# A decoder layer's last eight down products: parts of 384 and 128 tokens in place of two halves of 256

## What is computed

```python
h = h + 0.5 * swiglu(rmsnorm(h, ffn2_norm[layer]), ffn2_w_gate[layer], ffn2_w_up[layer], ffn2_w_down[layer])
...
h = rmsnorm(h, final_norm)
return h[:, N_META:]
```

## Time and profile before

| | us |
|---|---|
| median of 3 runs (lowest, highest) | 1050.07 (1049.4, 1050.22) |
| the profiled execution, its own time | 1049.71 |
| its span, first to last instruction | 1048.0 |
| TensorE busy in the span | 1036.8 |
| VectorE / ScalarE / GpSimd busy | 741.8 / 501.9 / 589.5 |
| the stage of the last eight down products | 1014.67 to 1039.84 of the span |

### The profile page before, as it was taken

How to read it: one execution, slowest core, us unless ns; L and a number is a source line. 1 busy time by engine, 2 the same in 40 slices (tenths; PEclk the granted TensorE clock), 3 DMA queues, 4 the chain that set the end, 5 groups by cost and what they waited for, 6 DMA issues and landing times.

```text
span 1048.0 us, 20252 instructions
## 1 busy us (share of the span) xinstructions
PE 1036.8 (99%) x7723; PEld 961.8 (92%) x7723; DVE 741.8 (71%) x1271; ACT 501.9 (48%) x838; POOL 589.5 (56%) x695
## 2 busy tenths in 40 slices
PE   9999999999999999999999999999999999999997
PEld 9999999999999999879867787778899999999997
DVE  7547786566675588699875584578988876776735
ACT  6444455445354354562455526454554553554435
POOL 5945776575564367269821304356767755655740
PEclk9999999999999999989999999999999999999999
DMA  7245455555554444336311101222444655555532
GB/s 204 86 111 143 112 125 133 141 125 128 151 127 104 133 116 116 85 101 160 84 42 42 42 21 61 81 71 81 115 114 119 162 136 143 146 116 151 126 77 81
DMA packets 188772, 115.52 MB, mean 110 GB/s; under 512 B 7939, under 2 KB 178998, under 8 KB 188678
## 3 DMA queue, kind: packets, MB, share of 16 engines
q1 hardware_dynamic: 178208, 97.38, 33.0%
q0 software_dynamic: 10368, 16.78, 9.5%
q10 hardware_dynamic: 102, 0.08, 0.1%
HBM read 91.18 MB, written 2.10 MB: 89 GB/s over the span
## 4 chain that ended last, share of the span: by engine, by line
PE 94%; DVE 2%; issue 1%; ACT 1%; POOL 0%; DMA 0%; DVEq 0%; ACTq 0%; POOLq 0%
PE ps L2563 44%; PE ps L2784 34%; PE ps L617 4%; PE ps L2599 2%; PE ps L806 1%; PE ps L755 1%; PE ps L785 1%; PE ps L923 1%; PE ps L2835 1%; PE ps L2810 1%; PE ps L964 0%; POOL wl L1862 0%; PE ps L698 0%; DMA wxl<-raw 0%; DVE mask L1411 0%
## 5 line engine op out<-in xcount | busy, mean ns | idle before, releaser
L1862 POOL TENSOR_TENSOR wl<-raw,wh 128x256 fp32r<-128x256 f32 x292 | 248.0, 892 | 200.3 <-ACT wh L1997 165.2
L1884 POOL DMA_DIRECT2D wxl<-raw x72 | 60.7, 843 | 188.4 <-ACT wxl L2002 188.4
L2563 PE MATMUL ps<-ah,wxh 128*128 128x264 f32 (+2 forms) x464 | 123.2, 319 | 0.6 <-DMA wxl<-raw 0.6
L2563 PE MATMUL ps<-ah,wxl 128*128 128x264 f32 (+2 forms) x464 | 123.0, 318 | 0.0
L2563 PE MATMUL ps<-al,wxh 128*128 128x264 f32 (+2 forms) x464 | 122.8, 318 | 0.0
L2563 PE MATMUL ps<-xh,wh 128*128 128x264 f32 (+3 forms) x432 | 122.2, 334 | 0.2 <-DVE pja L1505 0.2
L1862 POOL TENSOR_TENSOR wxl<-raw,wxh 128x256 fp32r<-128x256 f32 x112 | 109.6, 1012 | 19.2 <-ACT wxh L1997 19.2
L2563 PE MATMUL ps<-xl,wh 128*128 128x264 f32 (+3 forms) x432 | 117.9, 324 | 0.0
L2563 PE MATMUL ps<-xh,wl 128*128 128x264 f32 (+3 forms) x432 | 117.7, 324 | 0.0
L2328 DVE SCALAR_TENSOR_TENSOR h<-ps,h 128x528 f32<-128x528 f32 (+1 forms) x88 | 61.0, 695 | 62.0 <-PE ps L2563 61.5
L1997 ACT ACTIVATE wxh<-raw 128x512 fp32r<-128x512 f32 (+2 forms) x88 | 53.6, 609 | 105.1 <-PE ps L2563 103.1
(11 more groups left out here) (326 smaller groups left out, 3004.0 us busy)
## 6 DMA issues: line engine op xcount, KB each, us to landing
raw<-in_ffn_w_gate SPq DMA_DIRECT2D x44, 512.0 KB, 4.4
raw<-in_ffn_w_up SPq DMA_DIRECT2D x44, 512.0 KB, 4.7
raw<-in_ffn_w_down SPq DMA_DIRECT2D x80, 256.0 KB, 2.8
wxl<-raw POOLq DMA_DIRECT2D x56, 256.0 KB, 3.6
raw<-in_w_in SPq DMA_DIRECT2D x28, 512.0 KB, 4.4
raw<-in_w_out SPq DMA_DIRECT2D x8, 512.0 KB, 3.4
xin<-in_x SPq DMA_DIRECT2D x4, 512.0 KB, 5.9
raw<-in_ffn_w_down SPq DMA_DIRECT2D x16, 128.0 KB, 2.2
```

What stands on the lines that cost most here:

```text
L1862: op = pool.tensor_tensor(dst[:, part], src[:, part], high[:, part].bitcast(F32), ALU.subtract)
L1884: pool.dma_start(places(1, PLACE[u], 1)[:, 0:n], raw[:, u % RING, 0:n], accum_op=ALU.add).then_inc(low_added[e], 16)
L2563: mm = pe.matmul(ps[0:m, bank + a, 0:width], places(lo, PLACE[u], -(-WIDTH[u] // HALF_UNIT))[:, k * P:k * P + m], r[:, tile, t:t + width], ...
```

## The change

The tokens of the last eight down products are divided into parts of 384 (tiles 0, 1, 2) and 128 (tile 3) instead of 256 and 256 (`Y_TILES`, `y_width`, `y_part`). Adds, squares, scales and sums follow these widths; the first norm is for three tiles and the second for one (`y_norm`). The turns get a new order (`Y_TURNS`), with tile 2 turned among the second part's products, and the keeps are called with the tiles they take.

```diff
+        Y_TILES = [(0, 1, 2), (3,)]
+        Y_TURNS = [(0, 0), (1, 0), (0, 1), (1, 1), (2, 0), (2, 1), (3, 0), (3, 1)]
+        def y_width(a):
+            return P * len(Y_TILES[a])
         def y_part(i):
-            t = META + i // KT * (SEQ // 2)
-            return slice(t, t + SEQ // 2)
+            a = i // KT
+            t = META + P * Y_TILES[a][0]
+            return slice(t, t + y_width(a))
...
-        def keep_y(eng, half, a):
+        def keep_y(eng, half, a, tiles):
             eng.wait_ge(rstd_done, 4 + a)
-            for t in (2 * a, 2 * a + 1):
-                eng.wait_ge(y_turned, 4 * a + 2 * half + t % 2 + 1)
+            for t in tiles:
+                eng.wait_ge(y_turned, Y_TURNS.index((t, half)) + 1)
...
-                if i == KT + 2:
+                if i == KT + 3:
                     root_out(0)
-                elif i == KT + 4:
-                    keep_y(act, 1, 0)
+                elif i == KT + 5:
+                    keep_y(act, 1, 0, (0, 1))
             scale_half(2 * KT - 2)
             scale_half(2 * KT - 1)
+            keep_y(act, 1, 0, (2,))
             root_out(1)
-            keep_y(act, 1, 1)
+            keep_y(act, 1, 1, (3,))
...
-                if i == KT + 2:
+                if i == KT + 3:
                     variance(0)
-                elif i == KT + 4:
-                    keep_y(dve, 0, 0)
+                elif i == KT + 5:
+                    keep_y(dve, 0, 0, (0, 1))
+            keep_y(dve, 0, 0, (2,))
             variance(1)
-            keep_y(dve, 0, 1)
+            keep_y(dve, 0, 1, (3,))
...
-                    pe.wait_ge(y_done, 8 * (t // 2) + 4 * half + k + 1)
+                    pe.wait_ge(y_done, 8 * (t // 3) + 4 * half + k + 1)
...
-                for c in (2 * a, 2 * a + 1):
+                for c in Y_TILES[a]:
...
-                                       [(a, META + a * SEQ // 2, SEQ // 2)], tiles[0] - first)
+                                       [(a, y_part(a * KT).start, y_width(a))], tiles[0] - first)
...
                 for d in range(3):
                     part(1, d, 2, cnt)
-                    if d == 1:
-                        turn_out(0, 0, 0, 4)
-                        turn_out(1, 0, 0, 4)
+                turn_out(0, 0, 0, 4)
+                turn_out(1, 0, 0, 4)
+                part(1, 3, 0, cnt)
                 token_sums(0)
-                for d in range(3, KT):
+                for n, d in enumerate(range(4, KT)):
                     part(1, d, 0, cnt)
-                    if d == 3:
-                        turn_out(0, 1, 0, 4)
-                    elif d == 4:
-                        turn_out(1, 1, 0, 4)
+                    turn_out(*Y_TURNS[2 + n], 0, 4)
...
-            turn_out(2, 0, 0, 4)
             turn_out(3, 0, 0, 4)
-            turn_out(2, 1, 0, 3)
             turn_out(3, 1, 0, 3)
             token_sums(1)
-            turn_out(2, 1, 3, 4)
             turn_out(3, 1, 3, 4)
```

More of the change, by code:

```diff
@@ L493, in build, with y_norm @@
         SUM_BANK = [6, 1]
+        Y_TILES = [(0, 1, 2), (3,)]
+        Y_TURNS = [(0, 0), (1, 0), (0, 1), (1, 1), (2, 0), (2, 1), (3, 0), (3, 1)]
+        def y_width(a):
+            return P * len(Y_TILES[a])
         def y_part(i):
-            t = META + i // KT * (SEQ // 2)
-            return slice(t, t + SEQ // 2)
+            a = i // KT
+            t = META + P * Y_TILES[a][0]
+            return slice(t, t + y_width(a))
+        def y_norm(a):
+            return slice(Y_TILES[a][0], Y_TILES[a][-1] + 1)
         def y_bank(t, half):
             return (0, 2, 4, 6)[t % 2 + 2 * half]
-        def keep_y(eng, half, a):
+        def keep_y(eng, half, a, tiles):
             eng.wait_ge(rstd_done, 4 + a)
-            for t in (2 * a, 2 * a + 1):
-                eng.wait_ge(y_turned, 4 * a + 2 * half + t % 2 + 1)
+            for t in tiles:
+                eng.wait_ge(y_turned, Y_TURNS.index((t, half)) + 1)
                 src, dst = ps[:, y_bank(t, half), :], xin[:, t, 512 * half:512 * half + 512]
@@ L2206, in root_out @@
                 act.wait_ge(inv_done, 4 + a)
-                act.activation(rout[:, 2 * a:2 * a + 2], rout[:, 2 * a:2 * a + 2], ACT.Sqrt).then_inc(rstd_done, 1)
+                act.activation(rout[:, y_norm(a)], rout[:, y_norm(a)], ACT.Sqrt).then_inc(rstd_done, 1)
             for i in range(2 * KT):
@@ L2515, in add_half @@
                 part = h[:, d, y_part(i)]
-                dve.scalar_tensor_tensor(out=part, in0=ps[:, down_bank(last, d, 1) + a, 0:SEQ // 2], scalar=0.5, in1=part,
+                dve.scalar_tensor_tensor(out=part, in0=ps[:, down_bank(last, d, 1) + a, 0:y_width(a)], scalar=0.5, in1=part,
                                          op0=ALU.mult, op1=ALU.add).then_inc(h_done, 1)
@@ L2526, in variance @@
                 dve.wait_ge(norm_sum, 4 + a)
-                part = rout[:, 2 * a:2 * a + 2]
-                dve.tensor_scalar(part, ps[:, SUM_BANK[a], 2 * a:2 * a + 2], 1.0 / D, EPS, ALU.mult, ALU.add).then_inc(var_done, 1)
+                part = rout[:, y_norm(a)]
+                dve.tensor_scalar(part, ps[:, SUM_BANK[a], y_norm(a)], 1.0 / D, EPS, ALU.mult, ALU.add).then_inc(var_done, 1)
                 dve.wait_ge(var_done, 4 + a)
```

## The result

The changed kernel takes 1053.43 us, the kernel before 1049.05 (medians of 20 runs each). The medians differ by 4.4 us. The ratio is 1.0053, with a 95% interval of 1.0037 to 1.0069, which is 5.6 us (3.9 to 7.2) slower. The lowest times, 1050.03 and 1045.1, differ by 4.9. The direction was as forecast. The size was not: the forecast was 15.8 us, and the measured time lies in the range only because that reached down to rival A. The profiled execution of the changed kernel took 1054.67 us, its span is 1052.8, against 1048.0.

A forecast was written before the change was run, and what follows sets the result against it. The prediction took TensorE's products and the tail behind them to bound the kernel. Its terms, +16.4 for products, +1.3 for a wait and -1.9 for the tail, gave +15.8 us: 1065.9 us, range 1052.2 to 1068.0.

The forecast's parts named there:

- rival A: Narrow second-part products: the load of 128 weight columns sets their pace, 0.09 to 0.108 us each, +3.8 us net; chance 0.25.
- Step 1: First part of the last down products: 96 products of 384 columns at 0.175 us, 16.8 us.
- Step 2: Second part of the last down products: 96 products of 128 columns at 0.232 us, 22.3 us.
- the four passes: Narrow second-part products occupy the array as long as 512 columns do, 0.232 us each, without a second load; chance 0.57.
- second leg of step 2: Index scores, line 696: widening block 0's 128 keys to 256 columns taken as a hint that narrow rounded products are dear.
- Step 3: Last down products: 192 products of 256 columns removed, 22.75 us; products together +16.4 us.
- Step 4: TensorE waits before tile 2's turn, behind d = 6, for VectorE's keep of tile 0: +1.3 us.
- Step 5: Turns moved among or right at the products cost TensorE what they did before; no other wait binds.
- Step 6: Tail behind the last product: 1.4 us won up to the last keep, 0.5 at the last store, -1.9 us together.
- B: Narrow second-part products: columns alone set the price, load hidden, 0.062 us each, -0.6 us net; chance 0.12 with prices to 0.085.
- C: Narrow second-part products run as plain ones with a second load, 0.29 to 0.32 us each, +21 to +24 us net; chance 0.06.

The follow-up runs named there:

- the plain kernel: The changed kernel with the 96 products of the second part reading the same numbers as plain f32: 0.224 us a product, stage 48.9 us against 38.1.

## Why the prediction was right or wrong

**What bounds the kernel** was read rightly: TensorE was never idle in the stage, and the time followed its products and the tail.

**Step 1, 384 columns**: 0.175 us forecast, 0.1746 measured.

**Step 2, 128 columns**, is where it failed. It took 0.232 us, "for as long as 512 columns do", since "the only 4-byte products of 128 columns in the trace are the plain ones". Measured: 0.112. The term was 22.3 us and is 10.8, which is 11.5 us of an error of 10 to 11; the smaller slips below go both ways. What failed is the transfer from plain to rounded operands, and with it the four passes. The rounded type runs in one record a product at any width in these runs, 64 to 512, and its price doesn't follow the columns from 192 down. That plain products of 128 columns, at 0.224 us in the plain kernel, come near the 0.232 is no support for the four passes: it is two records of 0.112 us each, the step of the narrow products beside them.

Two readings of rows were off as well. The 0.29 to 0.32 us of the earlier trace rows come from four records behind an idle stretch and are not the price in a stream, 0.224. Nor are they the only plain products of 128 columns in the trace: those of lines 884 and 918, in the fences above, take 0.125 to 0.128 us in two records. The 0.09 us of the earlier trace rows end with a start that was early. The product behind the four transposes started at 1033.43, and the next one 0.20 us later instead of 0.12:

```profile
1033.63 0.28 PE L2563 MATMUL ps<-al,wh 128*128 128x256 f32 x1
```

From the first transpose, at 1033.07, to there it is 0.56 us in 5 steps, 0.112 each.

The rows that carried the answer were in the earlier trace rows: transposes with the same load, 0.108 us for the ten. I set them aside because they multiply nothing; what they share with the products, 128 weight columns each, was the very thing that bound. Rival A had the price and the mechanism right: it gave +3.8 us against 4.8 in the spans.

The section LDWEIGHTS of the Trainium skill's page "TensorE: Matmul & The Clock Gate" has a load take its columns / 1.2 ns, by which 128 weight columns come to an estimate of 107 ns and 64 to half of it. This case shows 111 ns from start to start with 128, and 61 with 64, where the stream of 128 columns may be what binds; it was the rule to follow. The 81 ns that the Trainium skill's section Back-to-back issue gap on that page has for a load and a product of 128 columns are not seen here: it is 111 with weights of 128 by 128, and 62 a record at line 918.

A second leg of step 2 was false too: the code does not "stay clear" of 128 columns at line 696. It was read from one line, without the list that calls it.

**Step 3**, products together: +16.4 forecast, +4.5 measured. The 192 products taken out were worth 23.1 us and not 22.75, since the first one behind a turn or a sum is slower.

**Step 4**, the wait: +1.3 forecast, 1.24 us of idling and 1.40 from start to start measured, at the place and with the releaser named.

**Step 5**, moved turns at no cost: too good. The turn of tile 2 and the sums of a third tile stand ahead of the last product now, +0.75 us, and the tail's term, which I had taken along VectorE, already contained the gain of having less work there.

**Step 6**, the tail: -1.9 forecast, -1.92 measured. From the end of the last product to the end of the last keep it is 2.94 us (1046.54 to 1048.73 + 0.75), 3.05 forecast, and from there to the end of the span 3.3, 3.2 forecast. The range's upper end, added up again from its parts, is 1067.7 and not 1068.0; nothing hangs on that.

**Rivals.** B, columns alone: its price shows up only when the weight columns are halved, and then the stage is 33.4 us, as before. C: second records appear only with the plain type. With the measured sizes put in, the prediction's sum is 16.8 + 10.8 - 23.1 + 1.4 + 0.75 - 1.9 = +4.75, the difference of the stages. The times' 5.6 (3.9 to 7.2) agree with that; the clock's fall behind the wait, seen in one of the changed kernel's two profiles, would add to it, but how much of the rest it is was not measured.

## What to carry to other kernels

Before a matrix product is made narrower, compare its price by columns with the load of its weights. Here, with 128 weight columns each, moving the split of 512 tokens off the middle should cost nothing while both parts keep some 240 columns (an estimate: there the line of the wide products meets 0.111 us); below that, every product pays the load, and the products of a split of 384 and 128 cost a fifth more than those of 256 and 256. When the trace lacks the operation, look for the row that shares the suspected resource, not the one that shares the type's name. And work moved out of a tail lands ahead of it: count it in both places.

## What the runs showed of the hardware that I had not expected

A rounded 4-byte product with weights of 128 rows by 128 columns has a floor that its own columns don't move: 0.111 us from start to start at 64, 128 and 192 columns, and one-column products of plain f32 keep the same step between records. With 64 weight columns the step at 128 columns is 0.061. The load's own record lasts 0.19 us for 128 weight columns and 0.13 for 64: longer than the steps, so the records of loads overlap and are no price. Where the weights fill 64 rows, the two halves in turn, the step is 0.062 with 128 weight columns (line 918), so the floor is not a matter of weight columns alone. And the granted clock fell from 1.00 to 0.50 (2.4 to 1.2 GHz) right behind 1.24 us of idling in one of the five profiles that entered such a stretch at 1.00, and once among 64-column products without any idling, in a stage whose clock stayed at 1.00 to the last product in every profile but these two.
